# 44 of 128 expert tiles handled densely in place of 40, with one-hots built for four tokens at a time in place of eight

## The reference, cut to what matters

```
i = i1 * 128 + i2                       # best 16 of the pairs, per token and head
u = take(u_tab, ix)                     # rows of 2048 floats
act = gelu(einsum('chkd,cd->chk', u, hx))
vv = take(v_tab, ix)
y = einsum('chk,chkd->cd', gx * act, vv)
```

## Time and profile before

| | |
|---|---|
| median of 3 runs | 1755.9 us (1754.61 to 1756.68) |
| the profiled execution's own time | 1757.74 us |
| its span, first to last instruction | 1756.0 us |
| mean granted TensorE clock | 0.911 |
| busy: PE, DVE, POOL, ACT | 84%, 69%, 40%, 31% of the span |
| moved by DMA | 624.46 MB, 356 GB/s on average |

### The profile page before, as it was taken

The page is one execution under the profiler, slowest core; times in us unless marked ns, Lnnn a source line. Parts: engine busy times, 40 slices in busy tenths (PEclk is TensorE's granted clock), DMA queues, the critical chain, the costliest instruction groups (busy, mean ns, idle before and its releaser), DMA issues.

```text
span 1756.0 us, 20157 instructions
## 1 busy us (share of the span) xinstructions
PE 1476.3 (84%) x7320; PEld 977.8 (56%) x7320; DVE 1204.6 (69%) x2134; ACT 543.5 (31%) x1589; POOL 703.4 (40%) x626
## 2 busy tenths in 40 slices
PE   2979999989999998898899757756699898988865
PEld 1648987878788875666676434424343333333321
DVE  5877886889889988898454477768644545454462
ACT  3003432764311256343210146436411010110132
POOL 1001011000122344555666567556643555454461
PEclk9979999999999999999999966767799999999888
DMA  9999997849969679999999999998999999999996
GB/s 337 386 386 406 403 376 305 308 175 369 356 225 359 233 302 372 379 372 391 358 406 375 357 372 394 343 377 325 376 356 392 359 402 395 352 415 412 406 353 257
DMA packets 149806, 624.46 MB, mean 356 GB/s; under 512 B 33994, under 2 KB 38272, under 8 KB 86528
## 3 DMA queue, kind: packets, MB, share of 16 engines
q0 software_dynamic: 82976, 427.52, 62.4%
q1 hardware_dynamic: 66732, 195.67, 29.1%
HBM read 797.54 MB, written 2.10 MB: 455 GB/s over the span
## 4 chain that ended last, share of the span: by engine, by line
PE 39%; DMA 23%; DVE 22%; issue 6%; POOL 6%; ACT 3%; DVEq 1%; SPq 1%; POOLq 0%; ACTq 0%
DMA u_rows<-in_peer_u,expert 12%; DVE u_rows L2030 10%; PE ps L1216 8%; PE ps L1164 7%; DMA v_rows<-in_peer_v,expert_rows 7%; PE ps L457 5%; PE ps L1066 5%; PE ps L909 4%; POOL v_rows L800 4%; DVE first_acc L486 3%; PE ps L903 2%; PE ps L1131 2%; DMA ada_first<-in_w_ada 2%; DMA dense_rows<-in_dense_v 1%; DVEq L1950 1%
## 5 line engine op out<-in xcount | busy, mean ns | idle before, releaser
L2030 DVE SCALAR_TENSOR_TENSOR u_rows<-u_rows,h 128x1024 f32<-128x1024 f32 (+1 forms) x416 | 593.5, 1467 | 379.9 <-DMA u_rows<-in_peer_u,expert 365.4
L800 POOL DMA_INDIRECT u_rows<-in_peer_u,expert x256 | 333.8, 1304 | 348.0 <-DVE u_rows L2030 265.8
L800 POOL DMA_INDIRECT v_rows<-in_peer_v,expert_rows x210 | 278.5, 1326 | 193.5 <-PE ps L1164 140.1
L1164 PE MATMUL ps<-v_rows,diag 128*32 128x512 f32 x1680 | 266.8, 704 | 84.9 <-DMA v_rows<-in_peer_v,expert_rows 75.8
L1216 PE MATMUL ps<-dense_rows,dense_weight 128*128 128x512 f32 x640 | 286.5, 605 | 13.7 <-DVE dense_sums L2109 6.6
L457 PE MATMUL ps<-h2T,dense_rows 128*128 128x256 f32 x1280 | 284.2, 383 | 3.8 <-ACT dense_weight L1562 3.8
L457 PEld LDWEIGHTS ps<-h2T,dense_rows 128*128 128x128 f32 x1280 | 243.5, 191 | 52.3 <-issue 16.1
L1216 PEld LDWEIGHTS ps<-dense_rows,dense_weight 128*128 128x128 f32 x640 | 121.7, 193 | 178.1 <-issue 169.0
L1164 PEld LDWEIGHTS ps<-v_rows,diag 128*32 128x32 f32 x1680 | 68.1, 126 | 229.8 <-issue 229.4
L308 POOL DMA_DIRECT2D ada_late<-in_w_ada x61 | 32.3, 530 | 304.4 <-DVE ada_acc L322 262.5
L322 DVE SCALAR_TENSOR_TENSOR ada_acc<-ada_late,cact,ada_acc 128x2048 f32<-128x2048 f32 x57 | 133.8, 2348 | 17.1 <-DMA ada_late<-in_w_ada 15.9
(11 more groups left out here) (308 smaller groups left out, 1842.8 us busy)
## 6 DMA issues: line engine op xcount, KB each, us to landing
ada_late<-in_w_ada POOLq DMA_DIRECT2D x61, 1024.0 KB, 7.8
dense_rows<-in_dense_u SPq DMA_DIRECT2D x40, 1024.0 KB, 18.3
dense_rows<-in_dense_v SPq DMA_DIRECT2D x40, 1024.0 KB
ada_first<-in_w_ada SPq DMA_DIRECT2D x64, 512.0 KB, 11.7
ring<-in_w_in SPq DMA_DIRECT2D x10, 2048.0 KB, 24.7
ring<-in_w_o SPq DMA_DIRECT2D x8, 2048.0 KB, 15.0
ring<-in_w_peer_q SPq DMA_DIRECT2D x8, 2048.0 KB, 14.7
opened<-in_w_in SPq DMA_DIRECT2D x8, 1024.0 KB, 13.0
```

Source lines behind the costliest of these rows:

```text
L800: nc.gpsimd.indirect_dma_start(buf[:, :], None, table, bass.IndirectOffsetOnAxis(ap=places, axis=0), bounds_check=last_sparse, oob_is_err= ...
L1164: ins = nc.tensor.matmul(ps[rows, k, :], diag[n % len(diag)][:, :], v_slot(n)[0][:, 512 * k:512 * k + 512], start=first, stop=last)
L2030: ins = nc.vector.scalar_tensor_tensor(out=u_rows[b][:, lo:hi], in0=u_rows[b][:, lo:hi], scalar=1.0, in1=h2[:, q // H, lo:hi], op0=ALU.mul ...
```

## The change

The 40 dense tiles become 44 (`DENSE`, and with it `SPARSE` = 84 and the bounds of every gather), so four tiles' picks leave the gathers and four more tiles are loaded, scored, gated and multiplied. Batches are of 4 tokens in place of 8 (64 in place of 32), which frees room for the four tiles' weights. The keys are set anew: tiles at 22 + 15i/8, batches at 107 + 9i/10, products at 167 + 19j/10. PE's spreading of the gain row (`g2b`) at step 146 comes behind the batches of that step.

```
-DENSE = 40
+DENSE = 44
-BATCH = 8
+BATCH = 4
...
-    dense_weight = [at("dense_weight0", B + 16 * KB, [P, 28, T]), at("dense_weight1", C + 16 * KB, [P, 8, T]), at("dense_weight2", B + 12 * KB, [P, 4, T])]
-    WEIGHT_TILES = 0, 28, 36, 40
-    low_hot = [at(f"low_hot{b}", B + 4 * b * KB, [P, BATCH, NK]) for b in range(2)]
-    high_hot = [at(f"high_hot{b}", B + 8 * KB + 1280 * b, [P, BATCH, DENSE]) for b in range(2)]
-    slot_rows = at("slot_rows", B + 8 * KB + 2560, [P, 3, P])
+    dense_weight = [at("dense_weight0", B + 16 * KB, [P, 28, T]), at("dense_weight1", C + 16 * KB, [P, 8, T]), at("dense_weight2", B + 8 * KB, [P, 8, T])]
+    WEIGHT_TILES = 0, 28, 36, 44
+    low_hot = [at(f"low_hot{b}", B + 2 * b * KB, [P, BATCH, NK]) for b in range(2)]
+    high_hot = [at(f"high_hot{b}", B + 4 * KB + 704 * b, [P, BATCH, DENSE]) for b in range(2)]
+    slot_rows = at("slot_rows", B + 4 * KB + 1408, [P, 3, P])
...
     def tile_key(i):
-        return 22 + 2 * i
+        return 22 + 15 * i // 8
     def batch_key(i):
-        return HOT_KEY + 9 * i // 5 + (3 if i >= BATCHES else 0)
+        return HOT_KEY + 9 * i // 10 + (3 if i >= BATCHES else 0)
     def piece_key(j):
-        return 166 + 21 * j // 10
+        return 167 + 19 * j // 10
...
-                if n == G2_KEY:
-                    pe.wait_ge(experts_ready, QJOBS)
-                    spread_row("g2b", modc, G2)
...
                 for i in due(batch_key, TT * BATCHES, n - 1):
                     scattered(i)
+                if n == G2_KEY:
+                    pe.wait_ge(experts_ready, QJOBS)
+                    spread_row("g2b", modc, G2)
```

## The result

The changed kernel takes 1778.5 us, median of 4 runs (1774.8 to 1783.4), against 1755.3 for the kernel before beside it: a ratio of 1.0134, 95% interval 1.0111 to 1.0156, or 23.5 us more. The forecast was 12 us more, 1768 us, range 1746 to 1786. The way was right and the size about half.

What follows compares the result with a forecast made beforehand. Bytes and PE work were taken to bind stages A and C together, only B having PE time to spare. A +3, POOL's wait +8, B -3, C +7, tail -3 make +12 on 1755.9: 1768 us, range 1746 to 1786.

Steps and rivals of the forecast that it cites:

- Bytes: Gathers lose 4.94% of their bytes, dense loads grow: net A -1.7, B -11.9, C -3.6, tail -2.6, together -20 us.
- Stage A's PE work: Row groups with dense-tile scores: three heavy cycles (three tiles) lose 7.6 us each, most regained; with bytes +3 us.
- POOL's wait: End of stage A: a gather needing a dense-tile buffer waits for the last scores, now 4.30 us; cost +8 us.
- those 17 us: End of stage A: two tiles more (14 us) and one late load (2.9), mostly idle DMA; half taken, +8.
- Stage B: Token batches between scores and products: bytes -11.9 us, DVE's fixed costs +9, together -3 us.
- A third of the 26 us: Stage B: smaller batches add 26 us of DVE fixed costs, partly hidden by waits for gathered rows; +9 counted.
- The coupling: Stage B: one-hots wait for PE's batch two before, now 1.8 steps old, formerly 3.6; DVE may stall sooner.
- Stage C: Dense products: four more, 28 us against 37 us of PE idle, three more late loads, bytes -3.6: +7 us.
- Rival 1: PE's idle time hides the four tiles and the bytes count: about -8 to -12 us, 1745 us; chance 0.22.
- Rival 3: PE paces stages A and C from end to end: +30 us, 1786 us; chance 0.12.
- Rival 4: Stage B: all 26 us of DVE work on the path, +14 in place of -3, 1785 us; chance 0.08.
- The clock variant: Variant of rival 1: a PE that idles less is quicker, by up to 2.5 us at some five places.

Runs made afterwards that it cites:

- run 3: Kernel before, but its gathers also leave out the picks of tiles 84 to 87, with no dense tile added: ratio 0.9868, -23 us.
- run 5: Kernel before with four more tile scores and their loads at the change's steps; gathers, batches and products as before: ratio 1.0111, +19.5 us.
- run 6: Kernel before with four more products and their loads at the change's steps; gathers, scores and batches as before: ratio 1.0081, +14 us.
- run 10: Kernel before with four more tile scores that use rows already loaded, so without the 4.2 MB of loads: ratio 1.0106, +19 us.
- run 7: Changed kernel with the tiles' scores four steps earlier (18 + 15i/8): ratio 1.0114 to the kernel before.
- run 8: Changed kernel with tile keys 14 + 2i, pairs throughout and no gap with three tiles: ratio 1.0110 to the kernel before.
- run 11: Kernel before with batches of 8 tokens, each DVE instruction of a batch cut into halves of 4 tokens: ratio 1.0004.
- run 2: Kernel before with 40 tiles and only the change's batches of 4, g2b behind them, first product at step 167: ratio 1.0053, +9.3 us.

## Why the prediction was right or wrong, point by point

- **What bounds it: right.** PE's work and the bytes bind A and C together: either one changed alone moves the time (runs 3, 5, 6 and 10). The single parts add up: batches +9.3, scores +19.5, products +14.2, bytes -23.2 make +19.8, known to about 9 us, against 23.5 for the whole.
- **Bytes: the step that was mis-sized.** The sum valued every net byte at 416 GB/s, -20 us in all. Taken gross that is the gathers' 16.7 MB at -40 and the dense loads' 8.4 MB at +20. Written out like this the prediction's sum is A 23 (5 + 8, and 10 for loads), B 9, C 21 (11 and 10), gathers -40: +12. The runs have A 19.5, B 9.3, C 14.2, all with their loads, and gathers -23 (-16 with 44 tiles). So the added work with its loads was priced too high by some 10 us, and the saving by 17 to 24. That the forecast had the right way and half the size rests on two errors that partly cancel. Priced at what the DMA would need for them, the bytes were taken to count in full where PE is near its limit too, although the text itself says that both bind.
- **Stage A's PE work and POOL's wait: right in kind, too low where it counts.** Without bytes the prediction gave 13 us, and run 10 measured 19 for the work without its loads. The first part held: "most comes back before the next heavy one" is what the row groups of run 5 show, with some 5 us left by group 16. The late load was given as 2.9 us and measured 1.95 and 2.39. The part that failed is the stage's end: of "those 17 us" it says "I take half: +8", for some would be given back in B. Dots 96 to 104 take 12 to 19 us longer in the four kernels with the new tile keys and the gathers' buffers as they were, and B gives nothing back. That this is the price of POOL's wait as such isn't shown: in runs 7 and 8 the wait was shortened by moving tiles and the time stayed.
- **Stage B: size right by luck, cause wrong.** "A third of the 26 us" of DVE's fixed costs gave +9, and +9.3 was measured. But the fixed costs alone cost 0, -3 to +5 (run 11). The coupling, which the text named and gave no price, is the likely cause; run 2 less run 11 holds it with ACT's forms and two small shifts. The whole of stage B was to come out at -3, with 12 us of bytes saved, and did not: in the profile it is 1 us longer from dot 104 to 168, 8 more for the batches in run 2, 8 less for the bytes in run 3.
- **The page on fixed costs.** The Trainium skill, page "VectorE: DVE Perf Modes", section on the trn2 errata, warns of fixed costs per instruction. The sizes agree with the trace (338 and 345 ns for the 176-element forms of the changed kernel, against an estimated 341 by its formula), but here they lay in waiting time, and the rule changed nothing.
- **Stage C: PE's work near, its loads too high.** +7 with -3.6 of bytes in it is 10.6 for PE, or 21 with the 10 us that the sum gives the loads; +14.2 was measured for the work with its loads. C with 44 tiles became PE's. One of the five gaps with three products, from its third product on,

```profile
1597.61 7.13 PE L1216 MATMUL ps<-dense_rows,dense_weight 128*128 128x512 f32 x16 [1.73 <-DMA dense_rows<-in_dense_v]
```

  and PE's waits for gathered rows in C are 2.6 us in one place, where they had been 23 in six.
- **The rivals.** Rival 1 (idle time hides the tiles) falls with runs 5, 6 and 10. Rival 3 (PE paces both stages, 1786 us) looks closer to the result than the forecast, but its own terms don't add up to its +30: 45 less 3 for B, 3 for the tail and 5 for the bytes of A and C is +34. Its 45 us for A and C are 34 in runs 5 and 6, and stage A's waits for gathered rows, 20.3 us in the changed kernel for 33.9, speak against PE pacing all of it. Rival 4 (DVE-bound) falls with run 11. The clock variant came true in part and wasn't enough: the granted clock is 0.922 for 0.911 over the span, and in A 1.00 for 0.97.

## What to carry to other kernels

Where two resources are both near their end, price a saving on the one by what the other allows: take the byte saving alone and the added work alone. 17.8 MB bought 23 us here where the DMA's full rate would make 43, and 16 with the work added, a difference that these runs can't tell from noise. Idle time of an engine in pieces of 2 to 3 us per cycle is not room for all of the lumps of 7 us: of 28 us of PE work, A hid about a third and C half. Where a queue waits for the last piece of an engine's work, look at the end of the stage: what stood late there was never made up. Halving a batch between double buffers halves how far the engines may run apart; halving it cost 9 us here, most likely for this, and DVE's doubled number of instructions cost none.

## What the runs showed of the hardware that I had not expected

Four dense tiles more cost stage A as much without their 4.2 MB of loads as with them (1.0106 and 1.0111), in a stage whose DMA share was 0.96. Its end came some 6 to 12 us earlier when 4.9 MB of gathers left it (run 3). So the share alone doesn't tell whether a given byte costs time. That the loads were free isn't shown: the two ratios leave 11 us either way.
